# Four subtractions of 256 columns in place of one of 1024 on GpSimd, in the splitting of each weight panel

## The reference

```python
for i in range(DEPTH):            # gqa, diff, mlstm, gqa
    h = rms_norm(x, norm_g[i]) * (1 + scale) + shift
    q, k, v, z = split(h @ w_in)
    o = mixer(q, k, v)
    x = x + gate * ((o * silu(z)) @ w_out)
```

## Time and profile before

| | |
|---|---|
| three runs | 2256.05, 2256.95, 2260.66 us; median 2256.95 |
| the profiled execution | 2252.97 us, its span 2251.2 us |
| mean granted TensorE clock | 0.948 of full speed |
| PE busy | 2058.2 us, 91% of the span |
| DVE, ACT, POOL busy | 1177.5, 803.4, 547.6 us (52%, 36%, 24%) |

### The profile page before, as it was taken

How to read it: one execution, slowest core, us unless ns; L and a number is a source line. 1 busy time by engine, 2 the same in 40 slices (tenths; PEclk the granted TensorE clock), 3 DMA queues, 4 the chain that set the end, 5 groups by cost and what they waited for, 6 DMA issues and landing times.

```text
span 2251.2 us, 34991 instructions
## 1 busy us (share of the span) xinstructions
PE 2058.2 (91%) x14168; PEld 1765.2 (78%) x14168; DVE 1177.5 (52%) x2309; ACT 803.4 (36%) x1824; POOL 547.6 (24%) x440
## 2 busy tenths in 40 slices
PE   6999998889999997979979999998997989999888
PEld 4887886878989886968957868687876977888677
DVE  5477665563555553576534323241161666777544
ACT  5365554123444443031132232313221035555432
POOL 1313200433233311334310111102112542222122
PEclk8999998989999998979979999999998989999889
DMA  9212122322223223134222334325236221102001
GB/s 330 56 49 78 51 59 80 89 59 80 66 81 98 63 62 115 38 51 154 81 61 71 91 121 103 94 87 143 93 96 132 68 77 30 51 2 69 20 20 57
DMA packets 302286, 181.53 MB, mean 81 GB/s; under 512 B 59557, under 2 KB 276910, under 8 KB 302126
## 3 DMA queue, kind: packets, MB, share of 16 engines
q1 hardware_dynamic: 283860, 158.39, 24.0%
q10 hardware_dynamic: 18266, 20.90, 4.1%
HBM read 153.51 MB, written 25.74 MB: 80 GB/s over the span
## 4 chain that ended last, share of the span: by engine, by line
PE 75%; DVE 9%; ACT 8%; DMA 3%; issue 3%; SPq 1%; ACTq 1%; POOL 0%; DVEq 0%; POOLq 0%
PE pc L1682 20%; PE acc L1608 12%; PE acc L710 5%; PE acc L1774 4%; PE acc L1763 4%; PE pt L1785 3%; PE acc L700 3%; PE pc L765 3%; PE pt L710 2%; PE acc L1992 2%; PE acc L2004 2%; DMA out_mlstm_n<-amat 1%; PE acc L654 1%; PE pt L2012 1%; PE acc L1938 1%
## 5 line engine op out<-in xcount | busy, mean ns | idle before, releaser
L1523 POOL TENSOR_TENSOR idle<-eps 128x1 f32<-128x1 f32 x144 | 38.1, 264 | 1637.8 <-PE pc L765 306.0
L1682 PE MATMUL pc<-hh,wh 128*128 128x320 f32 x1152 | 380.0, 330 | 16.7 <-DVE hl L2661 8.2
L1526 POOL TENSOR_TENSOR wl<-raw,wh 128x1024 fp32r<-128x1024 f32 x144 | 368.0, 2556 | 11.5
L1682 PE MATMUL pc<-hl,wh 128*128 128x320 f32 x1152 | 362.1, 314 | 0.0
L1682 PE MATMUL pc<-hh,wl 128*128 128x320 f32 x1152 | 361.9, 314 | 0.0
L1682 PEld LDWEIGHTS pc<-hh,wh 128*128 128x128 f32 x1152 | 221.8, 192 | 29.0 <-issue 15.7
L1682 PEld LDWEIGHTS pc<-hl,wh 128*128 128x128 f32 x1152 | 222.8, 193 | 0.2 <-issue 0.2
L1682 PEld LDWEIGHTS pc<-hh,wl 128*128 128x128 f32 x1152 | 221.9, 193 | 0.0
L2283 ACT COPY ht<-pt 128x512 f32<-128x512 f32 (+1 forms) x160 | 76.4, 525 | 214.8 <-PE pt L1785 214.6
L1524 POOL CAST wh<-raw 128x1024 fp32r<-128x1024 f32 x144 | 150.9, 1048 | 0.0
L1774 PE MATMUL acc<-ht,gvt 128*64 128x128 f32 x1344 | 100.7, 298 | 19.3 <-ACT ht L2288 14.9
(11 more groups left out here) (386 smaller groups left out, 4437.6 us busy)
## 6 DMA issues: line engine op xcount, KB each, us to landing
raw<-in_w_mod SPq DMA_DIRECT2D x144, 256.0 KB, 3.4
raw<-in_gqa_w_in SPq DMA_DIRECT2D x80, 256.0 KB, 3.6
raw<-in_diff_w_in SPq DMA_DIRECT2D x64, 256.0 KB, 3.8
raw<-in_mlstm_w_in SPq DMA_DIRECT2D x64, 256.0 KB, 3.4
praw<-in_w_mod SPq DMA_DIRECT2D x32, 256.0 KB, 9.9
raw<-in_gqa_w_out SPq DMA_DIRECT2D x32, 256.0 KB, 3.2
out_mlstm_C<-amat ACTq DMA_DIRECT2D x16, 512.0 KB, 7.4
raw<-in_mlstm_w_out SPq DMA_DIRECT2D x32, 256.0 KB, 3.1
```

The source lines that it names most:

```text
L1526: pool.tensor_tensor(wl[:, s], raw[:, r], wh[:, s].bitcast(F32), ALU.subtract).then_inc(w_full[s], 1)
L1682: ins = pe.matmul(pc[:, c:c + 320], w[:, sl, kt, :], h[:, kt, t:t + 320], start=kt == 0 and n == 0, stop=kt == KT - 1 and n == 2)
```

## The change

```diff
-                pool.tensor_tensor(wl[:, s], raw[:, r], wh[:, s].bitcast(F32), ALU.subtract).then_inc(w_full[s], 1)
+                for k in range(0, KT, 2):
+                    ins = pool.tensor_tensor(wl[:, s, k:k + 2], raw[:, r, k:k + 2], wh[:, s, k:k + 2].bitcast(F32), ALU.subtract)
+                ins.then_inc(w_full[s], 1)
```

## The result

The changed kernel takes 2238.70 us (median of six executions, 2233.21 to 2245.65) against 2257.03 for the kernel before beside it (2255.92 to 2260.66): a ratio of 0.992, 95% interval 0.990 to 0.994, or 18.3 us. Measured once more later (five executions) it took 2236.21, 0.991 (0.990 to 0.993). The forecast was 6 us, with 11 us as the most that its range held.

The account below looks back on a forecast made before the run. PE bounds the kernel, busy 2058.2 of 2251.2 us; POOL's subtraction matters only where holding DVE lengthens PE's pauses. Terms sum to -5.9 us, 2252.97 to 2247.1; with 4.0 up to the median, 2251 forecast, range 2246 to 2259.

Parts of the forecast that it names:

- DVE gets in: Between two pieces of a POOL subtraction a waiting DVE operation passes, held at most 0.54 us in place of 2.15.
- The first rival: The pieces run on without a gap, so DVE waits for all four, 0.45 us longer each: 2264, slower; chance 0.08.
- End of layer 0: PE idles 1.54 us for the held L2962, which would end 1.5 us sooner: -1.54.
- First scores of layer 3: PE idles 3.75 us behind ACT, which waits for the held L2757: -1.35, between -1.1 and -1.6.
- Last scores of layer 0: ACT's second exponential waits 0.76 us for L2757, and PE for ACT's copy behind it: -0.76.
- Last scores of layer 3: The same wait for L2757 with 0.82 us, where the second value may meet a piece: -0.55.
- End of the mlstm cells: L1242 and low parts L1326 are held; PE shows 0.89 us of this behind ACT's copies: -0.9, between 0 and -2.0.
- The one late panel: The panel for which PE waited 13.1 us has no cover, so its split's longer time adds +0.45 us.
- The eight panels there give 0: Head of the mlstm layer, DVE without pause: four operations each meet one piece, 2.14 us in place of 2.145, no gain.
- The clock: Behind layer 3's 3.75 us pause the granted clock was 0.50; getting some back gives 1.2 us, between nothing and 2.8.
- The rivals: Four: pieces run on as one (chance 0.08), a piece holds its whole 0.73 (0.12), pauses filled up (0.20), more comes back (0.12).
- more comes back: The mlstm chain whole (-2.0) and the clock behind the pause whole (-2.8): -8.6, 2248; chance 0.12.

Follow-up runs that it names:

- lateness alone: The kernel before, subtraction uncut, with three more one-element POOL operations ahead of each cast: 2257.31 us, ratio 1.000 (0.998 to 1.001).

## Why the prediction was right in kind and short by two thirds

**DVE gets in: right.** A held L2759 takes 0.70 us, 0.54 of hold for a piece of 0.736, as worked out. The Trainium skill (SBUF - State Buffer, section Who interferes with whom) has the port pair held for the whole instruction; the hold measured is 0.2 us shorter. The first rival (pieces run on as one) would have made L2757's longest 2.7; it is 0.99, and that one is held by a whole cast (393.39 and 393.45 above), which the change leaves alone; with the cast in four the longest is 0.77.

**The pauses that were named: right, with two misses.** End of layer 0: -1.54, measured -1.54. First scores of layer 3: -1.35, measured -1.37. Last scores of layer 0: -0.76 came, but 0.47 went again in the block before, where ACT now waits for the L2759 that a cast holds (394.48 above): -0.29. Last scores of layer 3: -0.55, measured 0.82 - 0.38 = -0.44. End of the mlstm cells: -0.9; the low parts L1326 fell from 3.28 to 2.56 as forecast, but PE's 0.89 only to 0.78: -0.11, plus 0.2 in a wait behind it, so PE showed less of that chain than was taken. The one late panel: +0.45 forecast, 13.0 for 13.1 measured. Together about -4.0 for -4.65.

**"The eight panels there give 0": a step that failed, -4.0.** The step took each of four DVE operations to be held for a whole piece, at `bd` and at `cv` alike. For `bd` that is so:

```profile
974.37 0.77 POOL L1527 TENSOR_TENSOR wl<-raw,wh 128x256 fp32r<-128x256 f32 x1
974.48 0.81 DVE L1099 TENSOR_TENSOR bd<-mc,wsm 128x128 f32<-128x128 f32 x1
...
978.74 0.77 POOL L1527 TENSOR_TENSOR wl<-raw,wh 128x256 fp32r<-128x256 f32 x1
```

An unheld `bd` takes 0.28, so the piece holds it for 0.53, as worked out. The first twelve `bd` took 7.12 us for 7.71 mostly because the eighth piece, at 978.74, falls on none of them: one hold fewer. The twelve of the next group, with four pieces on them, took 5.04 for 5.08. For `cv` the step was wrong: four pieces held 1.56 us where one subtraction held 2.03, and, which the step did not look at, DVE got done before the next cast. That made the pause before L600 1.32 shorter, three times, -4.0. (L611's 8.08 is now 7.50; it is 7.60 with whole subtractions in this layer too, so that is not counted.) -4.0 and -4.0 make -8.0; the idle time fell by 8.6. The difference is other pauses, which went both ways: three of 0.27 to 0.86 us in layer 0, ahead of L1820 (L1818 before), are gone, and so is one of 1.60 ahead of L776; others grew by 0.2 to 1.1.

**The clock, -1.2: the step that failed most.** It was priced at one place, behind the 3.75 us pause, and there it came about as forecast: the hundred matmuls from the first scores on took 1.0 us less (L1765's eight products 1.97 for 2.50). Everywhere else it was put at nothing, without a reason, and that was the error. All matmuls together took 11.2 us less in the profiled execution; over all executions 19.6 us of mean less 9 of idle time leave about 10. At 0.946, some 5% of the clock is withheld in this kernel, in many short stretches. The changed kernel got 0.4 of these 5 points back, the one with layers 0 and 3 in pieces 0.3 (0.4 in 94.6 of 2058 us of matmuls is 9 us, by estimate). The runs show that shorter holds bring it and that lateness alone does not; by what path it comes stays open.

**The rivals.** None of the four was the case; the nearest, "more comes back" (2248), had the right sign for the wrong reason: of its two terms the mlstm chain gave 0.3 of 2.0 and the clock behind the pause 1.0 of 2.8, and both terms that counted were elsewhere.

## What to carry to other kernels

Where a POOL operation with two SBUF inputs makes DVE wait, cut it: each piece lets a waiting DVE operation in, at a price of about 0.2 us of POOL per cut, and two pieces may give most of what there is. Do the same for the cast beside it; cutting both finer still, in eight, brought nothing more here. Don't price a pause of TensorE by its length alone: with the clock below its upper level in places, time on other engines came back twice, as idle time and as matmul time, and the second part could be told only from the mean clock of several executions, not from one profile.

## What was not expected of the hardware

The same piece of 0.736 us holds one DVE operation for longer than another: 0.53 us a `bd` and 0.54 an L2759, which start just behind it, but 0.36 an L1150, 0.42 an L2964 and 0.48 an L1148. The pieces among the L1150 had themselves waited for DVE (four took 1009.80 to 1014.51 there, 4.71 us, for 2.82 at 1854.68); that the shorter hold comes of this is not shown. A cast, which reads one input, holds DVE as well (0.99 us for an L2759 of 0.16), and cutting it gave another 6 to 10 us. And a pause of TensorE 1.4 us shorter at 1868 us went with 4.0 us less matmul time in the stretch from 2100 us on, through the granted clock (0.87 to 0.89).
